# One 128x128x384 f32 product of constants ahead of each gated level's small products

## The reference

```python
def _gated_linear_chunked(q, k, v, log_f):
    gc = jnp.cumsum(log_f, axis=3)
    def step(state, inp):
        q_n, k_n, v_n, g_n = inp
        diff = g_n[:, :, :, None, :] - g_n[:, :, None, :, :]
        decay = jnp.exp(jnp.where(causal, diff, -jnp.inf))
        scores = jnp.einsum('bhcd,bhsd,bhcsd->bhcs', q_n, k_n, decay)
        ...
```

## Time and profile before

| | |
|---|---|
| median of 3 runs | 2463.57 us (2463.51 to 2466.93) |
| the profiled execution | 2461.06 us, its span 2459.3 us |
| mean granted clock of PE | 0.972 |
| PE busy | 2359.7 us (96%), 14784 products |
| DVE busy | 1683.5 us (68%) |
| ACT busy | 681.1 us (28%) |
| transfers | 252.44 MB, 103 GB/s in the mean |

### The profile page before, as it was taken

One profiled execution on the slowest core, in us unless ns is written; L12 is line 12 of the kernel. 1 busy time (PEld: TensorE's weight loads), 2 busy tenths in 40 slices (PEclk: granted clock), 3 DMA queues, 4 the chain that ended last, 5 costly groups with the idle time before them and its releaser, 6 DMA issues. The chain is left out here.

```text
span 2459.3 us, 35706 instructions
## 1 busy us (share of the span) xinstructions
PE 2359.7 (96%) x14784; PEld 1911.8 (78%) x14784; DVE 1683.5 (68%) x2643; ACT 681.1 (28%) x1239; POOL 139.2 (6%) x128
## 2 busy tenths in 40 slices
PE   8998859999999999999999899999999999999997
PEld 6886658977888888887755688888888888888886
DVE  6674466756888865558888686666666886666653
ACT  2321363022211101424677503222102113222200
POOL 0000002001000011000211010000010001000001
PEclk9999679999999999999999999999999999999999
DMA  4220003412232364212200171222562541322341
GB/s 180 77 77 3 21 2 129 146 52 78 95 102 94 128 207 145 88 67 82 73 10 2 55 271 65 98 94 95 184 223 89 205 180 61 103 94 95 132 137 65
DMA packets 70193, 252.44 MB, mean 103 GB/s; under 512 B 7792, under 2 KB 8080, under 8 KB 69520
## 3 DMA queue, kind: packets, MB, share of 16 engines
q1 hardware_dynamic: 69744, 249.63, 29.9%
q10 hardware_dynamic: 288, 0.54, 0.1%
HBM read 248.04 MB, written 2.10 MB: 102 GB/s over the span
## 5 line engine op out<-in xcount | busy, mean ns | idle before, releaser
L385 PE MATMUL psum<-rounded_n,rounded_high 128*128 128x512 f32 x1856 | 739.0, 398 | 4.4 <-DVE rounded_n_low L539 1.8
L386 PE MATMUL psum<-rounded_n_low,rounded_high 128*128 128x512 f32 x1856 | 726.3, 391 | 0.0
L387 PE MATMUL psum<-rounded_n,rounded_ring 128*128 128x512 f32 x1856 | 726.2, 391 | 0.0
L339 DVE TENSOR_TENSOR rounded_ring<-ring,rounded_high 128x1024 fp32r<-128x1024 f32 (+1 forms) x360 | 445.7, 1238 | 43.5 <-ACT rounded_high L322 31.5
L385 PEld LDWEIGHTS psum<-rounded_n,rounded_high 128*128 128x128 f32 x1856 | 350.6, 189 | 85.2 <-issue 7.2
L386 PEld LDWEIGHTS psum<-rounded_n_low,rounded_high 128*128 128x128 f32 x1856 | 350.7, 189 | 76.5 <-issue 5.5
L387 PEld LDWEIGHTS psum<-rounded_n,rounded_ring 128*128 128x128 f32 x1856 | 350.4, 189 | 73.7
L337 DVE CAST rounded_high<-ring 128x1024 fp32r<-128x1024 f32 (+1 forms) x347 | 248.8, 717 | 187.3 <-PE psum L387 180.1
L385 PE MATMUL psum<-rounded_arena,rounded_high 128*128 128x512 f32 x720 | 281.3, 391 | 4.4 <-DVE rounded_ring L339 4.4
L387 PE MATMUL psum<-rounded_arena,rounded_ring 128*128 128x512 f32 x720 | 281.0, 390 | 0.0
L386 PE MATMUL psum<-rounded_arena,rounded_high 128*128 128x512 f32 x720 | 280.9, 390 | 0.0
(11 more groups left out here) (494 smaller groups left out, 2752.4 us busy)
## 6 DMA issues: line engine op xcount, KB each, us to landing
ring<-in_w_up SPq DMA_DIRECT2D x132, 512.0 KB, 3.3
ring<-in_w_down SPq DMA_DIRECT2D x48, 512.0 KB, 3.6
n_low<-in_mod_w SPq DMA_DIRECT2D x48, 512.0 KB, 5.4
arena<-in_mod_w SPq DMA_DIRECT2D x48, 512.0 KB, 5.1
ring<-in_w_ab_in SPq DMA_DIRECT2D x37, 512.0 KB, 3.3
ring<-in_w_mix_in SPq DMA_DIRECT2D x31, 512.0 KB, 3.4
ring<-in_w_sc_in SPq DMA_DIRECT2D x24, 512.0 KB, 4.8
ring<-in_w_down SPq DMA_DIRECT2D x24, 384.0 KB, 3.2
```

The costliest lines, as they stand in the source:

```text
L339: nc.vector.tensor_tensor(self.rounded(raw), raw, self.rounded(high), ALU.subtract).then_inc(self.weights_split, 1)
L385: self.nc.tensor.matmul(out, w_high, x_high, start=first, stop=False)
L386: self.nc.tensor.matmul(out, w_high, x_low, start=False, stop=False)
L387: return self.nc.tensor.matmul(out, w_low, x_high, start=False, stop=last)
```

## The change

In `use`, between the wait on `taken` and the call that makes the level's products, every use with 0 <= s <= 5 gets one more product: the identity (128x128) times the first 384 columns of a table of constants of the same first stage, written to the first bank of the use. It is a complete product (start and stop), and the level's own products overwrite what they need of it. Nothing reads the rest. `SMALL_LEVELS`, the semaphores and the other engines' streams stay as they are.

```diff
@@ -1479,6 +1479,7 @@
     RET_BANK = (G0, D0 + 2)
     z = k.z
     SMALL_LEVELS = 5
+    FILL = 3 * P
 
@@ -1783,6 +1784,9 @@
             if x == 0:
                 pe.wait_ge(ret_kept, 2)
             pe.wait_ge(taken, TURNS + x - (1 if u and 0 <= s < VALUES else 0))
+            if 0 <= s <= BIG:
+                nc.tensor.matmul(k.psum[:, room(u, s), 0:FILL], k.const("ident"), k.const("decay0")[:, 0:FILL],
+                                 start=True, stop=True)
             if s < BIG:
                 small(u, s)
             elif s == BIG:
```

## The result

| | before | after |
|---|---|---|
| median of 20 runs | 2462.83 us (2460.1 to 2466.97) | 2467.97 us (2463.08 to 2473.38) |
| the profiled execution | 2461.06 us | 2466.85 us, span 2465.0 |

The ratio is 1.0021, 95% interval 1.0015 to 1.0027: 5.1 us slower, where 1.6 us faster was forecast. The time lies inside the range of 2455 to 2469, just beyond 0.2% on the slower side, which was given a chance of 0.13. Two single executions of the experiments' rounds, of 3387 us (the kernel before) and 3957 us (six and eight fills), fell in a slow state, with mean granted clocks of 0.65 and 0.55, and enter no ratio.

What follows compares the result with a forecast made beforehand. Bound: the mixers' stage, in unit 0 a chain of PE and DVE taking turns, at 1.2 GHz. Unit 0 -1.3, unit 1 +0.1, unit 2 0, fetching -0.4: -1.6 us, 2462.0 us against 2463.57; range 2455 to 2469.

Steps and rivals of the forecast that it cites:

- the slower side: Rival: the fills bring no rise of the clock in unit 0; 2473 us, or 2470 if only unit 0 misses; chance 0.14.
- What bounds the kernel: Mixers' stage, 208 to 377 us: dense products follow, so a microsecond won or lost before 377 us should reach the end.
- Price of one fill: Every added product: holds PE 0.64 us at the upper clock level, 1.28 us at the lower.
- Unit 0, cost: Uses 1 to 6: five fills wholly on the path, use 4's partly covered; together 6.0 us.
- Fetching: Unit 0, PE's unexplained idle time of 2.5 us: a long fill ahead may cover some, 0.4 us of gain.
- use 4's fill: Unit 0: partly covered while DVE is occupied; costs 0.55 us at the lower level, nothing at the upper.
- Unit 0, return: Unit 0, clock up from the fourth or fifth fill: faster solves, crosses, outputs and values return 7.3 us.
- use 5's part: Unit 0, level up one use earlier: cheaper fill, faster small products, scan's first outputs and keys; 1.6 us more, half counted.
- Unit 1: Uses 11 to 16: net +0.1 us if fills keep the level up at 312 to 319 us, +2.5 without; +0.1 taken.
- Unit 2: Uses 20 to 25: fills stand ahead of waits for DVE, so 0; clock changes can shift the tail 1 us either way.
- Early rise: Rival: unit 0's first fill lifts PE to the upper level and later ones hold it; 2456.0 us, chance 0.26.

Runs made afterwards that it cites:

- six and eight: Against the kernel before: six full fills ahead of unit 1's big level and eight ahead of unit 2's, none ahead of the other levels; ratio 0.9996.
- the thin ones: Against the kernel before: unit 0's six fills only, 384 columns each, in a 32x32 corner of the array; ratio 1.0014.
- three and four: Against the kernel before: three full fills ahead of unit 1's big level and four ahead of unit 2's, none elsewhere; ratio 0.9988.
- all eighteen thin: Against the kernel before: all eighteen fills with the same 384 columns, but in a 32x32 corner of the array; ratio 1.0052.

## Why the prediction was wrong

**What bounds the kernel.** That a microsecond in this stage reaches the end fits: 6.7 us at 384 us are 5.7 in the span, and the missing 1.0 us is within the scatter of single executions.

**Price of one fill.** 0.64 and 1.28 us were taken; 0.84 and 1.58 were measured. The rows priced were a pair of half-width products. That a single fill between other tiles shows the loading of its weights, and the pair hides it, is the likely reason, but no run separates it. In unit 0 the 0.3 us come back in the 128 small records behind (1.48 us against 1.78); in unit 1 they don't (0.89 us for 64 records of 64x32 with and without a fill ahead). This is a term mis-sized by 0.2 to 0.3 us, and in unit 0 it nearly cancels at the lower level.

**Unit 0, cost.** Right in kind. Uses 1 to 3, 5 and 6 stood on the path, and 0.6 us of use 4's fill was covered (0.73 in the working). Fetching gave 1.4 us where 0.4 was taken, since the pauses behind 116 records vanished, and the small products 1.3 us more. With these off, the six fills cost about 5.0 us in the profile, where the working had 6.0 - 0.4 = 5.6; the thin ones, in which unit 0 stayed at the lower level, cost 3.5 us. The cost was near right.

**Unit 0, return: the step that failed.** "If PE is at the upper level from use 6 on, until the rise that happens at 302 us anyway", 6.5 us, and with half of use 5's part 7.3 us. The rise came where it was put, but 6.8 us later PE was back at 1.2 GHz, and L1814, L1758 and L1778 ran as before: of the 6.5 us nothing came, and of use 5's part 1.4 us. Instead of -1.3 us unit 0 cost +3.7 us. The argument asked what makes the clock rise and never what keeps it. The prices were right: with two fills a level the join, the solve and the cross took what the working gave them. The condition was wrong. What would have kept the level stays open: in the change it fell in the course of the sixth fill, and in two profiles with pairs it lasted some 10 us behind the last fill, over the same work.

A second premise failed with it, that the kernel before is at 0.50 until 302 us. Unit 0 without any fill was profiled in four more kernels (fills in unit 1, in unit 2, six and eight, three and four), and its rise came at 303.4, 292.0, 294.3 and 305.9 us. This is the earliest, with the level at 1.00 from 292 to 295.5 us:

```profile
286.00:295.00 9.00, 7.85 (x76) 5.75 (x72) 2.07 (x6) 5.35 (x8) 0.00 (x0) 0.67 0.00 0
```

So a part of the return comes in some executions for nothing. In the change the rise came at 308.8 us, 5.0 us into the values where it had been 2.0, and that cost 1.4 us more before unit 1 began. A smaller slip: the small products of use 5 were read as 1.85 us, those of another use; in the profile of before they took 1.55, so that 0.3 us was to be won there and not 0.6.

**Unit 1.** "+0.1 with the level, +2.5 without": PE was at 0.51 from 319 to 329 us, and the fills of uses 13 and 14 took 1.58 us each. The take of use 13 came 8.0 us late after 5.5 at the unit's start, so the second value, 2.5, was the right one up to there. Use 14 was called covered. In truth it stands ahead of the four norms' sums, and they ended late with it. Not in the working at all was the return at the norms' spreading, 5.12 us to 2.84: with it unit 1 ended 5.0 us late, 0.5 less than at its start, near the +0.1 by luck. In the profile with fills in unit 1 alone this return is missing (4.83 us), and that kernel is 2.6 us slower.

**Unit 2.** Zero was taken; the test of it alone leaves -1 to +3 us. Its waits did cover the fills: L1735 idled less and DVE ran 5.0 us late from beginning to end (its take at 358.35 before, 363.36 after). That the clock's falls could move its tail "by 1 us either way" was 1.7 us in this profile.

**The rivals.** *Early rise* fell: the first fill lifted nothing in any profile with single ones. The slower side came true in size half-way: five of unit 0's six fills ran at the lower level for all or nearly all of their time and little was returned, but its price of 9.5 us left out what the small products and the fetching give back, the 1.4 us of the clock and what unit 1 returned. The rule of the Trainium skill (TensorE: Matmul & The Clock Gate, "What's actually happening"), read as busy time alone, doesn't fit here either: with all eighteen thin, PE was busy 24.08 of 25 us at a granted clock of 0.50 (319 to 344 us), and with the full ones 19.40 of 23.60 us at 1.00 (329.4 to 353 us).

## What to carry to other kernels

Work added to lift a clock must be priced twice: its own time at the level that it starts from, and how long the level lasts behind it; a rise that ends before the costly work gives next to nothing back (1.4 us for 8.3 us of fills here). Put such work only into waits that the trace shows, count it at the lower level's price, and end it before the wait ends: eighteen ahead of every level lost 5 us, and seven sized like this lost none (3 us less by the ratio, with no change at the edge of the interval). And look at several profiles before reading one: unit 0 without any change to it lasted 38.4, 38.4, 40.4, 40.4 and 41.2 us here, because the clock rose and fell at other moments.

## What the runs showed of the hardware

- Busy PE is not enough for the upper level: with thin fills unit 0 was busy 33.07 of 37 us (tiles of 32x32 to 64x64, with a few solves and outputs over 128 rows) and the granted clock stayed at 0.50. With two full fills ahead of each level it was 1.00 from 266.5 to 300.6 us but for 3.5 us in one profile and from 267.5 to 298.2 in another; in a third, with the same unit 0, it rose at 276.3 and fell twice. Without any fill it rose once at 292 us, for 3.5 us. What makes it fall no run here shows.
- One product of 128x128 constants between tiles of another shape costs 0.3 us beyond its columns at the lower level: 0.73 us for 128 columns, 1.58 for 384.
- A long product ahead of the 32x32 products of unit 0 makes them faster: 128 records in 1.48 us from start to start, against 1.78, and without the pause behind the first 116. In unit 1, 64 records of 64x32 take 0.89 us with it and without.
